# A decoder layer with dense gate tables: who builds the one-hot rows of the odd batches, and how the last tables are stored

## What is computed

```python
def peer_retrieve(xn, w_query, sub_keys):
    q = (xn @ w_query).reshape(T, N_PEER_HEADS, 2, D_QUERY_HALF)
    s = jnp.einsum('thpc,hpkc->thpk', q, sub_keys)
    s1, i1 = lax.top_k(s[:, :, 0], PEER_TOPK)
    s2, i2 = lax.top_k(s[:, :, 1], PEER_TOPK)
    ...                        # 16 x 16 sums, the best 16 of them
    return idx, softmax(top_s) # idx = i1 * 128 + i2, 8 heads x 16 per token

def peer_experts(xn, idx, gates, expert_u, expert_v):
    u = expert_u[idx]; v = expert_v[idx]
    act = gelu(einsum('tkd,td->tk', u, x))
    return einsum('tk,tkd->td', gates * act, v)
```

## Time and profile before

| | us |
|---|---|
| median of three runs | 2589.92 |
| lowest and highest | 2584.86, 2595.16 |
| the profiled execution | 2585.36 |
| its span, first to last instruction | 2583.3 |
| PE busy in the span | 2485.5 (96%) |
| DVE busy | 1967.7 (76%) |
| POOL busy | 1438.9 (56%) |
| ACT busy | 430.4 (17%) |

### The profile page before, as it was taken

How to read it: one execution, slowest core, us unless ns; L and a number is a source line. 1 busy time by engine, 2 the same in 40 slices (tenths; PEclk the granted TensorE clock), 3 DMA queues, 4 the chain that set the end, 5 groups by cost and what they waited for, 6 DMA issues and landing times.

```text
span 2583.3 us, 23989 instructions
## 1 busy us (share of the span) xinstructions
PE 2485.5 (96%) x7573; PEld 1367.0 (53%) x7573; DVE 1967.7 (76%) x4240; ACT 430.4 (17%) x793; POOL 1438.9 (56%) x1169
## 2 busy tenths in 40 slices
PE   8999999999788899999999999999999999999998
PEld 6687785877666344444444444444444444444443
DVE  3308888788699779676888868778787777979788
ACT  1213313213787000010020000000000000000001
POOL 0000387587611257556666757666676766767664
PEclk9999999999999999999999999999999999999999
DMA  7553885865678889969999999999999999999997
GB/s 291 220 185 142 306 302 148 347 207 132 204 229 240 340 317 373 399 244 418 371 394 390 389 405 371 410 378 414 414 386 419 360 397 413 405 420 403 419 405 275
DMA packets 288061, 857.67 MB, mean 332 GB/s; under 512 B 42048, under 2 KB 99392, under 8 KB 273344
## 3 DMA queue, kind: packets, MB, share of 16 engines
q0 software_dynamic: 167184, 541.73, 55.4%
q1 hardware_dynamic: 108400, 289.25, 29.5%
q10 hardware_dynamic: 12352, 25.17, 2.6%
HBM read 807.75 MB, written 48.30 MB: 331 GB/s over the span
## 4 chain that ended last, share of the span: by engine, by line
PE 70%; POOL 8%; DMA 8%; DVE 5%; issue 4%; ACT 3%; DVEq 1%; ACTq 0%; SPq 0%
PE pairs L820 27%; PE pairs L774 27%; PE pairs L684 9%; DMA ring<-in_expert_u,idx 6%; POOL gate_tables L635 5%; POOL ring L664 4%; PE pairs L731 2%; PE pairs L706 2%; ACT arena L972 1%; PE pairs L787 1%; DVE junk L1173 1%; ACT pick_all L853 1%; DMA arena<-gate_tables 1%; DMA arena<-in_w_all 1%; ACT arena L996 1%
## 5 line engine op out<-in xcount | busy, mean ns | idle before, releaser
L664 POOL DMA_INDIRECT ring<-in_expert_u,idx x512 | 645.1, 1260 | 644.0 <-DVE dots L1173 391.1
L820 PE MATMUL pairs<-arena 128*128 128x512 f32 x2048 | 887.3, 595 | 14.7 <-DVE arena L1239 8.5
L774 PE MATMUL pairs<-arena 128*128 128x512 f32 x2048 | 882.5, 592 | 0.0
L1173 DVE CUSTOM_DVE_ANT_0 junk<-ring,xf 128x1024 bf16<-128x1024 f32 x512 | 612.8, 1223 | 196.0 <-DMA ring<-in_expert_u,idx 192.2
L664 POOL DMA_INDIRECT ring<-in_expert_v,idx x512 | 576.8, 1127 | 293.5 <-DVE arena L1184 134.1
L820 PEld LDWEIGHTS pairs<-arena 128*128 128x128 f32 x2048 | 390.4, 191 | 509.1 <-issue 501.3
L774 PEld LDWEIGHTS pairs<-arena 128*128 128x128 f32 x2048 | 388.6, 190 | 486.5 <-issue 486.5
L1184 DVE SCALAR_TENSOR_TENSOR arena<-ring,arena 128x1024 f32<-128x1024 f32 x381 | 474.3, 1281 | 107.5 <-DMA ring<-in_expert_v,idx 106.4
L684 PE MATMUL pairs<-arena 128*128 128x256 f32 (+1 forms) x1792 | 397.4, 385 | 9.0 <-ACT arena L927 5.3
L684 PEld LDWEIGHTS pairs<-arena 128*128 128x128 f32 x1792 | 344.0, 192 | 60.4 <-ACT arena L927 5.9
L980 ACT ACTIVATE arena<-pairs 128x512 f32<-128x512 f32 x128 | 76.3, 597 | 1177.5 <-PE pairs L774 1159.9
(11 more groups left out here) (169 smaller groups left out, 1093.8 us busy)
## 6 DMA issues: line engine op xcount, KB each, us to landing
arena<-in_w_all SPq DMA_DIRECT2D x80, 1024.0 KB, 6.4
arena<-in_uT SPq DMA_DIRECT2D x128, 512.0 KB, 7.8
arena<-in_expert_v SPq DMA_DIRECT2D x128, 512.0 KB, 9.6
arena<-gate_tables SPq DMA_DIRECT2D x32, 1024.0 KB, 9.1
gate_tables<-arena SPq DMA_DIRECT2D x11, 2048.0 KB, 9.7
gate_tables<-junk ACTq DMA_DIRECT2D x4, 2048.0 KB, 15.1
ring<-in_expert_u,idx POOLq DMA_INDIRECT x512, 9.2
ring<-in_expert_v,idx POOLq DMA_INDIRECT x512, 8.8
```

What stands on the lines that cost most here:

```text
L664: nc.gpsimd.indirect_dma_start(out=ring[:, r % RING, :], out_offset=None, in_=expert_u if table == "u" else expert_v, in_offset=bass.Indir ...
L774: last = nc.tensor.matmul(score_bank[x], uslot[:, x % USLOTS, k * P:(k + 1) * P], xfT[:, k, :], start=(k == 0), stop=(k == KD - 1))
L820: last = nc.tensor.matmul(o_bank[n % 4], gated[:, x % GSLOTS, t * P:(t + 1) * P], vrows[:, j, half * 512:(half + 1) * 512], start=(j == 0) ...
L1173: nc.vector.tensor_tensor_reduce(out=junk[:, r % 2, :], in0=row, in1=xf[:, t % 2, :], scale=1.0, scalar=0.0, op0=ALU.mult, op1=ALU.add, ac ...
```

## The change

The first one-hots are given out anew: DVE makes them for batches 0, 4, 8, ... (12 instead of 24), ACT for batch 1 and for 2, 6, 10, ... (13 instead of 24), and POOL for the odd batches from 3 on (23), in eight instructions of 128 x 128 each. POOL's are put into its program ahead of a row request: those of batch b ahead of the request of row `rows_then[b - 3] + RING`, where `rows_then[b]` is how many rows DVE has used after batch b. ACT's and POOL's one-hots have a semaphore each. The last tables are stored in three parts (2, 14 and 16 of the 32 groups), and `load_gates(1)` waits for the first two; the wait for the third comes behind it.

```diff
+        BY_ACT = [b for b in range(BATCHES) if b == 1 or b % 4 == 2]
+        BY_POOL = [b for b in range(BATCHES) if b % 2 == 1 and b > 1]
+        rows_then = [rows + sum(len(plan["hots", c]) for c in range(b + 1)) - sum(len(plan["hots", c]) for c in range(BATCHES)) for b in range(BATCHES)]
+        hots_before = {}
+        for b in BY_POOL:
+            hots_before.setdefault(rows_then[b - 3] + RING, []).append(b)
...
                     sp.dma_start(to[:, 0:2], of[:, 0:2]).then_inc(first_kept, 16)
-                    sp.dma_start(to[:, 2:], of[:, 2:]).then_inc(table_kept[c % STAGES], 16)
+                    sp.dma_start(to[:, 2:HALF_GROUPS // 2], of[:, 2:HALF_GROUPS // 2]).then_inc(next_kept, 16)
+                    sp.dma_start(to[:, HALF_GROUPS // 2:], of[:, HALF_GROUPS // 2:]).then_inc(table_kept[c % STAGES], 16)
...
+            sp.wait_ge(next_kept, 16)
+            load_gates(1)
             stage_kept(last_stage)
-            load_gates(1)
...
+            def first_hots(b):
+                c = b % HOTBUFS
+                pool.wait_ge(table_full, 2 * (b - HOTBUFS) + 2)
+                if b // (P // HOTS) > 0:
+                    pool.wait_ge(turned_out, b // (P // HOTS))
+                for t in range(HOTS):
+                    k = b * HOTS + t
+                    last = nc.gpsimd.tensor_scalar(hots[:, c, 0, t, :], iota[:], routeT[:, 0, k:k + 1], None, ALU.is_equal)
+                last.then_inc(hot_pool, 1)
...
                     r = HK * i + k
+                    for b in hots_before.get(r, ()):
+                        first_hots(b)
                     if r >= RING:
                         pool.wait_ge(rows_used, r - RING + 1)
...
-                if b % 2 == 1:
-                    pe.wait_ge(hot_first, b // 2 + 1)
+                if b in BY_ACT:
+                    pe.wait_ge(hot_act, BY_ACT.index(b) + 1)
+                elif b in BY_POOL:
+                    pe.wait_ge(hot_pool, BY_POOL.index(b) + 1)
...
-                if b % 2 == 1 and b + 2 < BATCHES:
+                if b + 2 in BY_ACT:
                     first_hots(b + 2)
...
-                if b % 2 == 0:
+                if b % 4 == 0:
                     nc.vector.tensor_tensor(hots[:, c, 0], iota[:].unsqueeze(1).to_broadcast([P, HOTS, KEYS]),
```

## The result

| | before | after |
|---|---|---|
| median | 2587.39 us (4 runs) | 2615.91 us (4 runs) |
| profiled execution | 2585.36 us | 2609.29 us |
| its span | 2583.3 us | 2607.5 us |
| POOL busy | 1438.9 us | 1549.4 us |

The changed kernel is slower: the ratio of the times is 1.0109, with a 95% interval of 1.0087 to 1.0131, or 28.5 us between the medians. The forecast was 2600 us and most likely no difference that can be told; the range of 2587 to 2626 us held the time, the likeliest case did not.

The account below looks back on a forecast made before the run. PE is full from 1200 to 2400 us, so the tables' stage ahead decides when it ends. Start +12.4, steady pace -2, stores -0.5: about +10 us on 2589.9, 2600 us, range 2587 to 2626.

Parts of the forecast that it names:

- What bounds the kernel now: PE is full from 1200 to 2400 us; the tables' stage decides, DVE's chain setting its 26.44 us period, ACT close behind.
- The start: First tables' batches: POOL's one-hots for batch 3 wait behind 80 scatters and seven row requests; tile 1 starts 12.4 us later.
- The steady pace: Four periods between score tiles 1 and 5: each gains 0.5 us, 2 us in all, with POOL's instruction at 0.4 us.
- Rival 1: Tables' stage: POOL becomes the bound from 0.585 us per instruction; at 0.7 us +27 us, 2617 us; chance 0.2.
- rival 2: Tables' stage: POOL and DVE take turns at the memory, costing DVE time; +28 us, up to +38 us; chance 0.2.
- The cost for DVE: Steady pace: each of POOL's 24 instructions in a period costs DVE 0.05 us, 1.2 us together.
- The stores: Last tables' stores in three parts: the second gates' load is issued earlier, gaining 0.5 us, between 0 and 1.2.
- Rival 3: Start and second gates: the start costs less, the gates' 8.1 us wait goes; -5.6 us, 2584 us; chance 0.1.
- Rival 4: Tables' stage: row requests between POOL's one-hots come late and DVE waits for rows; given no chance.

Follow-up runs that it names:

- pool_even: Kernel before, but POOL makes the first one-hots of batches 10, 14, 18, ..., ACT all odd ones, DVE the other even ones; ratio 1.0010.
- act_3_5: Changed kernel, but batches 3 and 5 get their first one-hots from ACT again and POOL starts with batch 7; 2600.12 us.
- pool_tt: Changed kernel, but POOL makes a batch's first one-hots in two instructions of 128 x 1024 instead of eight of 128 x 128; 2645.94 us.

## Why the prediction was wrong, point by point

**What bounds the kernel now** was right as far as it went. What the stage loses comes out at the end. But the chain of 26.44 us was ACT's and not DVE's: in the steady pace PE waited for ACT's copies alone, and pool_even, which relieves DVE, kept the 26.44. The waits of the earlier trace rows said so already, 16 pieces for ACT. I had ACT as "close behind", with DVE's chain of 25.9 us as the bound, and allowed up to 1.1 us for ACT's smaller share.

**The start** was right. The order of POOL's program was read correctly: batch 3 starts 33.7 us behind the first batch (predicted 697.5 - 665.1 = 32.4 us), PE had stood for 23.4 us, tile 0 comes at 41.4 us (predicted 706.2 - 665.1 = 41.1). Up to tile 1 it was +16.9 us, predicted +12.4. The 4.5 us between them arise behind tile 0, where I let PE run at its own pace and POOL held it up. The act_3_5 kernel gives 13 us in the stage as the price of the order.

**The steady pace** is the step that failed, and in it one term: the price of one of POOL's instructions. I took 0.4 us, near the select's 0.29 us, as "the same work on the same engine". It is 0.58 us alone and about 0.7 us in the mean beside DVE. The formula that I had for the rival gives 12.4 + 24 x 0.7 = 29.2 us for a period, and the trace has 29.54 us; the price from which it decides, 0.585 us, lies just below what was measured. So this term was not -2 us but +12.4 us. **Rival 1** was what happened, at the very price at which I had worked it out (c = 0.7: 2617 us, measured 2615.9), and I gave it a chance of 0.2 because of one row of another operation. The upper bound, 0.94 us of a row request, was nearer to the measured mean than the lower one.

The 0.7 us are two things, and the sum had only the first. With 0.594 us, the price beside short instructions, the formula gives 26.7 us, hardly more than before. The rest is POOL being kept out by DVE's instructions over 1024 columns: a batch takes 5.56 us in the mean where it takes 4.7 us without them, which for three batches is an estimated 2.6 us of a period's 3.1. The prediction put this at part of a tenth of a microsecond "for the operand and for DVE", and its rival 2 priced the turns at the memory in the other direction only. That I had worked rival 1 out at just 0.7 us was luck.

**The cost for DVE** was right: 0.05 us for each of POOL's instructions. DVE's eight took 2.31 us where it was 2.13, with three to four of POOL's in that time. **Rival 2**, the turns at the memory as a loss of DVE's, stays small with 128 columns each, and only POOL's long instructions in pool_tt show its price. In the changed kernel the turns cost POOL.

**The stores** were right in the main: 38.3 us from the store to the gates with the earlier issue, 38.1 us without, and no gain. In the changed kernel it was 36.2 us and not some 38. **Rival 3** is gone with that. **Rival 4**, late rows, did not occur: after the start DVE never waited for a row in this stage.

## What to carry to other kernels

Before work is moved to an engine, its price there needs a row of the same operation, not of a similar one; where the trace has none, work out the price from which the new engine becomes the bound (here 0.585 us), and if that lies between the bounds, the chance of it is large. The row has to be taken beside what the other engines do there, too: here a batch took 4.7 us beside short instructions and up to 6.6 us beside long ones. Read the receiving engine's whole program up to the moved piece: 80 scatters and seven requests stood ahead of it, and that alone cost 13 us. A wait that the trace puts down to one engine may be for another: here POOL's batches had ended 0.10 us before each. And relieving one of two nearly equally long chains moves nothing; here the only kernel that was faster relieved both and made POOL's part twice as cheap, by leaving half of it out.

## What the runs showed of the hardware

- On POOL a compare with a number costs 2.5 ns per column of 128 partitions and about 0.28 us besides (601 ns at 128, 1560 at 512, 2842 at 1024 columns). A subtraction of two inputs of 128 x 1024 takes 1.95 us, less than the compare with its one input.
- POOL and DVE keep one another out for whole instructions: 1.21 us of DVE became 3.60 us next to long instructions of POOL. One of POOL's 0.59 us became 2.54 us next to two of DVE's, of 1.21 and 1.22 us, over 1024 columns and with two inputs. With short ones on both sides DVE lost 8% (2.31 against 2.13 us for eight) and POOL next to nothing (4.74 against 4.67 us for eight).
